# Norms emitted one block ahead, earlier condition chunks, and two condition matvecs on TensorE

## The reference

```python
ada = c_act @ ada_w[l] + ada_b[l]                       # 1024 x 6144
sh1, sc1, gt1, sh2, sc2, gt2 = split(ada, 6)
h = rmsnorm(x, norm1_g) * (1.0 + sc1) + sh1             # norm 0
z = h @ w_in                                            # latents, conv input, gates
... attention, depthwise conv over 31 taps, w_out ...
h = rmsnorm(x, norm2_g) * (1.0 + sc2) + sh2             # norm 1
x = x + gt2 * hierarchical_moe(h, ...)                  # 32 experts
x = rmsnorm(x, final_norm_g)
for i in range(2):                                      # second block
    shift, scale, gate = split(silu(c_2) @ ada_w_2[i] + ada_b_2[i], 3)
    h = rmsnorm(x, norm_w_2[i]) * (1 + scale) + shift   # norms 2 and 3
    y = gdn_mixer(h, ...) if i == 0 else fox_mixer(h, ...)
    x = x + gate * y
return rmsnorm(x, final_norm_w_2)                       # norm 4
```

## Time and profile before

| what | us |
|---|---|
| median of 3 runs (lowest, highest) | 1217.89 (1216.08, 1219.47) |
| the profiled execution, its own time | 1220.97 |
| span of that execution in the trace | 1219.2 |
| TensorE busy | 1070.9 (88%) |
| VectorE busy | 639.4 (52%) |
| ScalarE busy | 491.9 (40%) |
| GpSimd busy | 398.6 (33%) |

### The profile page before, as it was taken

One profiled execution on the slowest core, in us unless ns is written; L12 is line 12 of the kernel. 1 busy time (PEld: TensorE's weight loads), 2 busy tenths in 40 slices (PEclk: granted clock), 3 DMA queues, 4 the chain that ended last, 5 costly groups with the idle time before them and its releaser, 6 DMA issues.

```text
span 1219.2 us, 20059 instructions
## 1 busy us (share of the span) xinstructions
PE 1070.9 (88%) x8110; PEld 925.1 (76%) x8110; DVE 639.4 (52%) x1382; ACT 491.9 (40%) x1100; POOL 398.6 (33%) x337
## 2 busy tenths in 40 slices
PE   2589778899899999999599989999889977999986
PEld 2487567788777777776588879899779866888865
DVE  7777976374434444545554535544454434455463
ACT  2434334322211011014386756836643533565542
POOL 0551334020000000101477464455433425554431
PEclk9699989799799999999699989999989978999988
DMA  9522451577089999731222222323221213323301
GB/s 349 212 91 109 142 203 35 234 267 297 1 337 353 406 387 400 294 133 74 103 104 97 79 70 71 104 70 106 70 70 39 102 37 123 117 107 113 131 35 35
DMA packets 25724, 186.22 MB, mean 153 GB/s; under 512 B 4128, under 2 KB 4768, under 8 KB 5536
## 3 DMA queue, kind: packets, MB, share of 16 engines
q1 hardware_dynamic: 24048, 184.77, 39.8%
q10 hardware_dynamic: 432, 0.18, 0.1%
q0 software_dynamic: 1152, 0.00, 0.0%
HBM read 196.46 MB, written 1.05 MB: 162 GB/s over the span
## 4 chain that ended last, share of the span: by engine, by line
PE 70%; DVE 18%; ACT 8%; issue 3%; DMA 2%; POOL 1%; DVEq 0%; ACTq 0%; POOLq 0%; SPq 0%
PE bank L666 67%; DVE arena L2092 5%; DVE sz L2092 2%; PE bank L670 2%; DVE arena L2089 2%; ACT wH L1489 1%; DVE hT L2092 1%; ACT arena L1489 1%; ACT xH L1486 1%; DVE wL L2089 1%; ACT arena L1486 1%; DVE xL L2092 1%; DVE arena L2095 1%; ACT tmpc L1486 1%; DMA ring<-in_exw,small 1%
## 5 line engine op out<-in xcount | busy, mean ns | idle before, releaser
L2916 POOL TENSOR_TENSOR wL<-ring,wH 128x512 fp32r<-128x512 f32 x210 | 279.8, 1346 | 336.2 <-ACT wH L1489 335.7
L666 PE MATMUL bank<-xH,wH 128*128 128x256 f32 x800 | 253.7, 317 | 33.5 <-DVE xL L2092 25.6
L666 PE MATMUL bank<-xH,wL 128*128 128x256 f32 x800 | 233.4, 292 | 0.0
L666 PE MATMUL bank<-xL,wH 128*128 128x256 f32 x800 | 232.6, 291 | 0.0
L666 PEld LDWEIGHTS bank<-xH,wH 128*128 128x128 f32 x800 | 160.4, 200 | 49.5 <-issue 34.7
L666 PEld LDWEIGHTS bank<-xH,wL 128*128 128x128 f32 x800 | 161.2, 201 | 4.7 <-issue 4.3
L1489 ACT ACTIVATE wH<-ring 128x512 fp32r<-128x512 f32 x264 | 154.0, 619 | 21.5 <-DMA ring<-in_wts 12.9
L666 PEld LDWEIGHTS bank<-xL,wH 128*128 128x128 f32 x800 | 160.4, 200 | 0.0
L666 PE MATMUL bank<-ring,xg 128*128 128x256 f32 x640 | 145.3, 380 | 2.6 <-DMA ring<-in_exw,small 1.5
L666 PEld LDWEIGHTS bank<-ring,xg 128*128 128x128 f32 x640 | 119.8, 190 | 24.5 <-issue 6.0
L2092 DVE SCALAR_TENSOR_TENSOR sz<-ring,cact,sz 128x512 f32<-128x512 f32 x168 | 132.1, 786 | 5.0 <-DMA ring<-in_wts 0.3
(11 more groups left out here) (201 smaller groups left out, 1831.7 us busy)
## 6 DMA issues: line engine op xcount, KB each, us to landing
ring<-in_wts SPq DMA_DIRECT2D x123, 1024.0 KB, 4.9
ring<-in_exw SPq DMA_DIRECT2D x32, 1536.0 KB, 8.9
ring<-in_wts SPq DMA_DIRECT2D x1, 1152.0 KB, 5.3
xT<-in_xT SPq DMA_DIRECT2D x1, 1024.0 KB, 13.5
out<-hT SPq DMA_DIRECT2D x4, 256.0 KB, 2.5
cst<-in_cst SPq DMA_DIRECT2D x1, 928.5 KB, 11.7
ring<-in_wts SPq DMA_DIRECT2D x1, 640.0 KB, 3.5
vec<-in_vec SPq DMA_DIRECT2D x1, 216.5 KB, 5.5
```

What stands on the lines that cost most here:

```text
L666: return pe.matmul(o, l, r, start=start, stop=stop, skip_group_check=True)
L2916: return pool.tensor_tensor(o, x, h.bitcast(F32), ALU.subtract)
```

## The change

Six edits.

1. **Matvecs 0 and 1 on TensorE.** `direct(j, x)` takes the chunk itself as the moving operand: the condition column `cact` is the stationary operand (128x1), the result one row of 512 in PSUM. ACT copies the row to SBUF, and `stand(j)` turns it into columns with four small products. DVE has matvecs 2 and 3 alone.
2. **Order and places of the first chunks.** `ada2a, ada0a, ada2b, ada0b, ada3a, ada1a, ada1b, cv0a, ada3b, cv0b`; `ada3a`, `ada1a`, `ada1b` lie at the start of the still idle arena (floats 20480 to 26624). The constants come in two parts: 256 columns early, 1600 after `cv0b`.
3. **Norms one block ahead.** DVE's order is y0, y1, l0, y2, l1, ... (`AHEAD`). Before norms 0 and 3 only one chunk is split; the pieces of the second (`cv0b`, `fqk0b`) are done inside the norm, one after each odd block.
4. **Sooner chunks.** In the expert stage each condition chunk stands one place earlier (`7 * u + 10`), which moves the places of all chunks; three get places by hand.
5. **Split of `gqk0a` and `gqk0b` inside the last steps** of the expert stage (ACT from u = 38, two pieces a step; DVE from u = 40), with a wait for the last chunks over `wH`/`wL` (`under_split`: `dn_p` 37, as `ov5` lies there, and matvec 23, row 3).
6. **Small moves.** `modulation(2)` to u = 30, `modulation(3)` ahead of the last recurrence step, the rotary work between matvecs, the two Sin calls behind norm 0, and the epsilon column into `vec`.

```diff
-    ada(0, 4)
+    for j, x in ((2, 0), (0, 0), (2, 1), (0, 1), (3, 0), (1, 0), (1, 1)):
+        half(j, x)
...
-        while h < 28 and 10 * h <= 7 * u:
+        while h < 28 and 10 * h <= 7 * u + 10:
...
+EARLY = ("ada3a", "ada1a", "ada1b")
+        at = {"ada3a": RING, "ov6": LONG - 3072, "ada2_1_5b": 10240, "ov7": RING}.get(name, at)
...
+AHEAD = [(0, "y")] + [(k + x, n) for k in range(8) for x, n in ((1, "y"), (0, "l")) if k + x < 8]
...
+        def under_split():
+            names = [n for n in WIDE if SPOT[n][0] < RING and 12288 < SPOT[n][1]]
+            return [freed_by([n for n in names if (n[:3] == "ada") == x][-1])[0] for x in (False, True)]
...
+            def direct(j, x):                                   # TensorE
+                name = f"ada{j}" + x
+                e.wait_ge(silu_c, 0)
+                e.wait_ge(loaded(name), name)
+                p = bank(3 + j) if x == "a" else banks[3 + j]
+                for i in range(4):
+                    k = 4 * (x == "b") + i
+                    m = mm(p[0:1, :], cact[:, k:k + 1], raw(name, 4)[:, i, :], k == 0, k == 7)
+                m.then_inc(ada_pe.up((j, x)))
+                until(3 + j, (ada_row, j))
...
                         if name[:4] == "gqk0":                  # ACT, high()
-                            e.wait_ge(dn_p, 39)
-                            e.wait_ge(ada_acc, (23, 7))
+                            for s, key in under_split():
+                                e.wait_ge(s, key)
...
+            for j in range(2):                                  # ACT, start
+                e.wait_ge(ada_pe, (j, "b"))
+                cp((tmpb, tmpc)[j][0:1, :], banks[3 + j][0:1, :]).then_inc(ada_row.up(j))
+                if j == 0:
+                    root(0, 0)
+            split.need("cv0a")
...
+                if 38 <= u:                                     # ACT, expert stage
+                    split.go()
+                    split.go()
...
             def normed(u, r, oh, ol, shift):                    # DVE
-                for k in range(8):
-                    stt(hT[:, k, :], ...)
-                    e.wait_ge(norm_a, (u, k))
-                    stt(ol[:, k, :], ...)
+                for k, n in AHEAD:
+                    if n == "y":
+                        stt(hT[:, k, :], ...)
+                    else:
+                        e.wait_ge(norm_a, (u, k))
+                        stt(ol[:, k, :], ...)
+                        if u in (0, 3) and k % 2:
+                            split.go()
```

More of the change, by code:

```diff
@@ L1397, in fox_head @@
                 yield
+            direct(0, "a")
+            direct(0, "b")
+            direct(1, "a")
             for k in range(8):
                 stat(0, k, 0)
-            each(chain(*[ada(j) for j in range(4)]))
+            direct(1, "b")
+            stand(0)
+            cols.append(2)
+            columns()
+            stand(1)
+            cols.append(3)
             columns()
@@ L1985, in scalar_program @@
             fn(cact[:, 8:16], vcol("c_2", 0, 8), ACT.Silu).then_inc(silu_c.up(1))
+            for k in range(8):
+                square(0, k)
+            for j in range(2):
[4 more added lines that the diff above has]
+            split.need("cv0a")
+            normed(0, xH2, lambda k: adaT[:, k:k + 1])
             for f, o in (("c", cosT), ("s", sinT)):
                 e.wait_ge(rope_d, (f, 7))
[L1988 to L1994 removed]
+                fn(o, rope_r[f], ACT.Sin).then_inc(rope_a.up(f))
             conv_in()
@@ L2035, in scalar_program @@
                 square(2, k)
-            split.need("gqk0b")
             exp_ln()
@@ L2064, in scalar_program @@
             each(out_proj("ao", 3, 3, True))
-            split.need("fqk0b")
+            split.need("fqk0a")
             root(3, 6)
@@ L2793, in fox_head @@
                 yield
-            positions()
-            each(chain(*[ada(j) for j in range(4)]))
+            pos_ = positions()
+            weave(ada(2), (pos_, 0.6))
+            weave(ada(3), (pos_, 0.6))
+            for j in range(2):
+                e.wait_ge(ada_col, j)
+                tt(adaT[:, 4 * j:4 * j + 4], banks[5 + j][:, 0:4], vcol("ada_b", 4 * j, 4), ALU.add).then_inc(ada_out.up(j))
             close()
-            split.need("cv0b")
+            split.need("cv0a")
             modulation(0, 8, 3, vcol("norm1_g", 0, 8))
@@ L2848, in vector_program @@
                     next(gad, None)
+                if u == 30:
+                    modulation(2, 56, 15, vcol("norm_w_2", 0, 8), vcol("final_norm_g", 0, 8))
                 if 2 <= u and (u - 2) % 8 == 7:
                     low_y((u - 2) // 8)
+                if 40 <= u:
+                    for _ in range(4):
+                        split.go()
                 if 11 <= u and (u - 11) % 8 < 4:
@@ L2855, in vector_program @@
                 scatter(4, i)
-            split.need("gqk0b")
-            modulation(2, 56, 15, vcol("norm_w_2", 0, 8), vcol("final_norm_g", 0, 8))
             e.wait_ge(root_a, (2, 1))
@@ L2889, in vector_program @@
             each(out_proj("ao", 3, 3, 64, True))
-            split.need("fqk0b")
-            modulation(3, 80, 23, vcol("norm_w_2", 8, 8))
+            split.need("fqk0a")
             e.wait_ge(mod_d, (3, 1))
```

92 lines of the change are left out of this document (58 added, 34 removed).

## The result

The changed kernel takes 1213.58 us (median of 20 runs, 1208.67 to 1218.2) beside 1220.91 for the kernel before in the same session (20 runs): ratio 0.9934, 95% interval 0.9914 to 0.9954. The medians lie 7.3 us apart, the ratio says 8.1 us (5.6 to 10.5). Forecast were 1204 and 14.2 us. The sign is right, the gain is about half of the forecast one, and the time lies just outside the range.

The account below looks back on a forecast made before the run. TensorE has 70% of the chain, so edits pay where it stands still or VectorE alone makes the end. Start 6.2, experts -1.3, experts' end with norm 2 4.8, norm 3 4.5: 14.2 off 1217.9, said 1204; range 1198 to 1213.5.

Parts of the forecast that it names:

- Start, forecast 6.2: Start through norm 0: streamed matvecs, new chunk order and y one block ahead gain 6.2 us.
- The stream's end: Start: TensorE finishes the streamed chunks and squares at 36.1 us, after 5.4 us at half clock.
- the second rival: Start: TensorE's stream runs at 1.2 GHz, y0 at 51, term -3.9 instead of +6.2, time 1213.8; chance 0.12.
- the norm from y0 on: Norm 0, y0 to last l: 8.9 us plus 1.0 for meetings with GpSimd, instead of 11.8.
- VectorE's own chain: Start: VectorE's matvec rows end at 36.8; column sums, adaT and two pieces follow, ending at 40.0 to 40.9.
- Behind it, up to 226 us: After norm 0 the same work runs on the same engines, so the start's 6.2 us stay in full.
- Experts, 1.3: Expert stage: sooner condition chunks make loads of the first experts late, 1.3 us lost, range 0 to 4.
- The third rival: Expert stage: each expert from 8 to 31 loads late, by 0.6 us eating the gain; 1223 at 0.8; chance 0.06.
- End of the experts, 3.0: Last expert steps: split delays silu of expert 39 by 2.6, VectorE's second piece adds 0.4; 3.0 lost.
- The fourth rival: Experts and norms: 6 us lost at the experts' end, 3 in the first ones, port waits double; 1211; chance 0.15.
- Norm 2, 7.8 behind the squares: Norm 2 after its sums of squares: split, table load and modulation gone, faster blocks; 7.8 us gained.
- Norm 3, 4.5 to the end of `forgets`: Norm 3: y0 3.4 us sooner, `forgets` ends at 1026.1 instead of 1030.6; gain 4.5, range 1 to 6.

Follow-up runs that it names:

- cols_first: Changed kernel with the column sums of matvec 2 ahead of the second chunk of matvec 1 in TensorE's list; 1211.96 us, ratio 0.991.
- before_piece: Kernel before with VectorE's split piece of in0b behind four convolution taps instead of eight; 1219.07 us, ratio 0.997.
- before_ahead: Kernel before with only VectorE's y one block ahead in norms 0, 2 and 3; 1210.33 us, ratio 0.9916.
- after_again: The changed kernel itself, nothing altered, measured and profiled once more; 1212.49 us, ratio 0.991.

## Why the prediction was wrong, step by step

- **Start, forecast 6.2.** Measured in place: 3.6. The stream's end was right (35.3 for 36.1), the second rival fell, and the norm from y0 on was right (9.7 for 9.9). The step that failed is "VectorE's own chain (36.8, column sums 0.9 to 1.86, adaT, two pieces for 1.9)": y0 came at 43.7 instead of 40.5. I followed VectorE's rows without the wait that `close()` puts between them, though the list of TensorE in the section on the change shows those sums behind the last streamed chunk. The wait took 3.78 us, and cols_first, which removes it, gives back 2.2 at y0. One load time of the sum was a lucky one: 5.8 MB at 351 GB/s and 2.4 us of latency make 18.9, not the 19.5 written; measured was 19.6.
- **"Behind it, up to 226 us, the same work follows on the same engines, so the 6.2 are kept."** It isn't a constant stretch. The meeting at 80 us holds 5 us and falls two ways. Of the 8.1 us between the two first traces, 4.8 are its outcome. They aren't work that the streamed matvecs save, and before_piece takes most of them with four taps moved; whether the new start makes the better outcome likelier (four of five against none of three) is open. The Trainium skill, "SBUF — State Buffer", says in "SBUF: two separate sides" that whichever instruction starts first gets the shared port pair for its whole length and the other is blocked. That is a rule for two instructions, and it leaves open which of two trains loses. VectorE's train had started 1.8 us earlier every time, and it lost in six of the ten traces with eight taps ahead of the piece.
- **Experts, 1.3.** 1.9 lost (7.9 to 6.0), and 1.5 gained ahead of expert 36, for which the kernel before had waited 1.47 us on an overflow load and the changed one didn't. The gain was not forecast. The third rival fell.
- **End of the experts, 3.0.** Measured 7.2, the largest error of size. The delay of the silu was named and priced nearly right: 2.9 at TensorE's transpose for 2.6. Against the other 0.4 stand 4.3: 2.2 at the column sums, 0.7 at `ysL` and 1.3 in products at half clock. The step that failed is that I priced ACT's and VectorE's part of the split and put GpSimd's six pieces, which now run beside the last matvec rows, at nothing; and VectorE's first piece, ahead of `ysL`, was not in the sum either. The fourth rival had 6 us for this place, and its 1211 was nearer than the forecast.
- **Norm 2, 7.8 behind the squares.** 8.5: right. **Norm 3, 4.5 to the end of `forgets`.** 4.8 (8.6 ahead at the last addition into xT, 13.4 behind `forgets`): right in place, but I booked it in full. 3.0 were gone in the next 31 to 34 us, in rows of half clock. before_ahead, with the same order but without the pieces, gains 3.3 in norm 3 and still has them there (31.3 us for this stretch, as in the kernel before). The 2.3 behind that are within what two traces of the kernel before differ by.

The sum by measured terms: 3.6 + 4.8 - 0.5 - 1.9 + 1.5 - 7.2 + 8.5 - 0.2 + 4.8 - 3.0 - 2.3 = 8.1; the 0.5 lie between 113 and 313 us, the 0.2 between 603 and 1006 us. So the result is half the forecast by several errors of both signs, and without the lucky outcome at 80 us this trace would have shown about 3 us, as after_again does (2.6). Not tried: the sooner chunks of edit 4 undone by themselves, since other places of the ring follow from them. What makes the clock rise late behind norm 3 isn't settled. The stretch behind `forgets` takes 34.4 to 35.3 us in all eight traces with split pieces inside norm 3, and 31.3 or 33.8 in the eight without.

## What to carry to other kernels

Before pricing a move on one engine, write down for every engine that shares the moved work what now stands beside it; the pieces on GpSimd that were out of the way behind the squares cost 2.2 us at once beside VectorE's last rows, and more in the half clock behind the wait. A gain at a wait is a gain only until the next stretch at half clock: book norm-sized gains with a discount, and look at the mean clock behind them. And before crediting a change with a stage it doesn't touch, profile both kernels twice.

## What the runs showed of the hardware

- The same two trains of instructions of VectorE and GpSimd, met at 1.79 us of distance, give 6.29 and 5.63 us or 3.25 and 7.47 us, in two executions of one program; 5.5 us lie between the spans of the two executions.
- A single GpSimd piece beside a norm in VectorE's old order stretches a y from 0.48 to 1.49 us, and with three engines in turn the delay is passed on: norm 0 takes 14.7 us from y0 to the last l, with two such meetings and the slower steps around them, and 11.8 without pieces.
- Streaming a 1 MB chunk through TensorE as the moving operand takes 3.59 us at full clock for eight records, with waits of 1.4 us between chunks and a granted clock of 1.00 up to 33.6 us. The very first chunk took 6.23 us, 0.78 a record, in the same stretch of granted 1.00: after 11.9 us of nothing on TensorE the records were slow where the granted clock doesn't show it.
- The granted clock of one stretch differs between executions with the same work in it: 0.64 over 10 us in one trace and 1.00 in another, for the same 24 products in 7.23 or 5.43 us.
